# Eight sample rows as the third instead of the second tile in the last stage of a decoder layer

## What is computed

```python
x = layer_norm(DN_ALPHA * x + ffn, lw['ln2_g'], lw['ln2_b'])
ple = jax.nn.sigmoid(x @ lw['w_ple_gate']) * (p.astype(x.dtype) @ lw['w_ple_proj'])
x = x + rms_norm(ple, lw['ple_norm_g'])
```

## Time and profile before

| | us |
|---|---|
| median of 3 runs | 970.74 (970.61 to 971.94) |
| profiled execution: time | 969.24 |
| profiled execution: span | 967.4 |
| TensorE busy in the span | 928.9 |
| VectorE busy | 427.4 |
| ScalarE busy | 246.9 |
| last stage, from the first turn to the end of the span | 893.2 to 967.4 |

### The profile page before, as it was taken

One profiled execution on the slowest core, in us unless ns is written; L12 is line 12 of the kernel. 1 busy time (PEld: TensorE's weight loads), 2 busy tenths in 40 slices (PEclk: granted clock), 3 DMA queues, 4 the chain that ended last, 5 costly groups with the idle time before them and its releaser, 6 DMA issues.

```text
span 967.4 us, 13929 instructions
## 1 busy us (share of the span) xinstructions
PE 928.9 (96%) x5256; PEld 553.3 (57%) x5256; DVE 427.4 (44%) x981; ACT 246.9 (26%) x531; POOL 96.8 (10%) x146
## 2 busy tenths in 40 slices
PE   8999999999999999999999999989999999897997
PEld 6777777777777766655678645443333333233344
DVE  0311467867634238687631243682111211013784
ACT  1122221132145015665730000131111111011335
POOL 0111211211211100000000000001221111110000
PEclk9999999999999999999999999999999999899999
DMA  9876888998797711011114892348999999999501
GB/s 374 340 250 230 283 310 308 327 335 291 274 350 256 277 44 47 28 39 42 66 32 171 348 422 103 136 176 325 421 422 422 423 423 426 421 418 363 220 24 65
DMA packets 65418, 247.38 MB, mean 256 GB/s; under 512 B 11302, under 2 KB 12207, under 8 KB 56359
## 3 DMA queue, kind: packets, MB, share of 16 engines
q1 hardware_dynamic: 46742, 191.29, 50.8%
q0 software_dynamic: 13216, 35.28, 10.0%
q10 hardware_dynamic: 5392, 19.93, 5.4%
HBM read 240.85 MB, written 18.05 MB: 268 GB/s over the span
## 4 chain that ended last, share of the span: by engine, by line
PE 76%; DMA 13%; DVE 6%; ACT 2%; issue 1%; SPq 1%; DVEq 0%; ACTq 0%; POOLq 0%
PE ps L902 20%; DMA arena<-in_wexp 10%; PE ps L1371 8%; PE ps L1291 6%; PE ps L1393 4%; PE ps L1220 4%; PE ps L990 3%; PE ps L961 3%; PE ps L1075 3%; PE ps L893 3%; PE ps L1496 3%; PE ps L1099 2%; PE ps L1039 2%; PE ps L1056 1%; PE ps L965 1%; PE ps L1505 1%
## 5 line engine op out<-in xcount | busy, mean ns | idle before, releaser
L902 PE MATMUL ps<-arena 128*128 128x260 f32 x928 | 214.3, 386 | 2.2 <-DMA arena<-in_xT 1.7
L902 PEld LDWEIGHTS ps<-arena 128*128 128x128 f32 x928 | 172.7, 190 | 37.2 <-issue 8.8
L1371 PE MATMUL ps<-arena 128*64 128x512 f32 x576 | 129.2, 601 | 9.7 <-DMA arena<-in_wexp 8.1
L1371 PEld LDWEIGHTS ps<-arena 128*64 128x64 f32 x576 | 42.1, 138 | 84.3 <-issue 81.8
L1869 DVE SCALAR_TENSOR_TENSOR arena<-arena,vec 128x512 f32<-128x512 f32 x120 | 81.7, 745 | 0.0
L2550 POOL DMA_DIRECT2D arena<-in_kv x96 | 51.7, 539 | 264.9 <-issue 258.8
L1393 PE MATMUL ps<-arena 128*64 128x512 f32 x288 | 65.8, 598 | 4.1 <-DMA arena<-in_wexp 4.1
L2376 DVE TENSOR_TENSOR arena<-ps,arena 128x256 f32<-128x256 f32 x18 | 7.6, 425 | 127.3 <-ACT arena L1727 127.3
L1291 PE MATMUL ps<-arena 128*128 128x512 f32 x128 | 58.4, 601 | 0.0
L1220 PE MATMUL ps<-arena 128*128 128x260 f32 x224 | 49.3, 382 | 0.0
L1220 PEld LDWEIGHTS ps<-arena 128*128 128x128 f32 x224 | 42.6, 190 | 6.5
(11 more groups left out here) (356 smaller groups left out, 1146.2 us busy)
## 6 DMA issues: line engine op xcount, KB each, us to landing
arena<-in_wexp SPq DMA_DIRECT2D x26, 2048.0 KB, 26.3
arena<-in_kv SPq DMA_DIRECT2D x160, 272.0 KB, 9.4
arena<-in_wexp SPq DMA_DIRECT2D x36, 1024.0 KB, 27.3
arena<-in_kv POOLq DMA_DIRECT2D x96, 272.0 KB, 7.4
arena<-in_w ACTq DMA_DIRECT2D x35, 512.0 KB, 7.4
arena<-in_wexp SPq DMA_DIRECT2D x16, 512.0 KB, 10.8
arena<-in_wo SPq DMA_DIRECT2D x8, 512.0 KB, 3.8
arena<-in_w_out SPq DMA_DIRECT2D x4, 1024.0 KB
```

The lines of the kernel that those rows point to most:

```text
L902: y = mm(ps[:, b + h, 0:TH], w[:, k], xT[:, k, h * TH:(h + 1) * TH], start=(k == 0), stop=(k == KD - 1))
L1371: y = mm(ps[64 * x:64 * x + 64, 2, :], xgT[:, k, 64 * x:64 * x + 64], wx[slot][:, x, k * 512:(k + 1) * 512], start=(k == 0), stop=(k == KD ...
```

## The change

The order becomes `ORDER2 = [0, 1, 4, 2, 3]`: place 1 is the full tile 1, place 2 the sample rows. On TensorE the first tile's last chunk is followed by the full product of place 1, with the next turn before its chunk 6; `narrow` is done for place 2, with `turn_x2(3)` straight behind it; and `narrow_sum` goes before chunk 4 of place 3, into banks 0 and 1 where it was 2 and 3. On VectorE the copy to `nparts` moves from before `last(0)` to behind `gated(1)`. ScalarE's and SyncE's code is the same; what they handle follows `ORDER2`, the loads too.

```diff
-ORDER2 = [0, 4, 1, 2, 3]
+ORDER2 = [0, 1, 4, 2, 3]
...
-                if u >= 2 and u != 3:
+                if u >= 3:
+
                     pe.wait_ge(s_hg, u - 1)
-                if u == 1:
-                    narrow(6, lambda k: fbT[:, 1, k, 0:32], lambda k: plg[k]).then_inc(s_np, 1)
-                    turn_x2(2)
+                if u == 2:
+                    narrow(6, lambda k: fbT[:, 0, k, 0:32], lambda k: plg[k]).then_inc(s_np, 1)
+                    turn_x2(3)
                 elif u < TILES - 1:
...
-                        if k == KD // 2 and u == 2:
+                        if k == KD // 2 and u == 3:
                             pe.wait_ge(s_npc, 1)
-                            narrow_sum(2, nparts, 1).then_inc(s_h, 1)
-                        if k == KD - 2 and u >= 2:
+                            narrow_sum(0, nparts, 1).then_inc(s_h, 1)
+                        if k == KD - 2 and u > 0:
                             turn_x2(u + 1)
-                        if k == 0 and u == 3:
-                            pe.wait_ge(s_hg, 2)
...
             gated(0)
-            dve.wait_ge(s_np, 1)
-            v.tensor_copy(nparts, ps[:, 6:8, :].rearrange("p h n -> p (h n)")).then_inc(s_npc, 1)
             last(0)
             front(3)
             gated(1)
+            dve.wait_ge(s_np, 1)
+            v.tensor_copy(nparts, ps[:, 6:8, :].rearrange("p h n -> p (h n)")).then_inc(s_npc, 1)
             last(1)
```

## The result

The changed kernel takes 982.14 us (median of 4 runs, 981.14 to 982.44), the kernel before 970.67 us in the runs beside it. The ratio is 1.0127, with a 95% interval from 1.0114 to 1.0141: it is slower by 12.3 us (11.1 to 13.7). Executions of one kernel spread by some us, and their mean granted clock with them: of 31 executions of the kernel before on one chip, those with a mean clock of 0.992 took 967.63 to 969.43 us, those with 0.987 took 971.95 to 973.61 us. The forecast was 978.6 with 974.5 to 981.0. The direction was right; the time lies outside the range, and the loss is half as large again as the 7.9 us forecast.

The account below looks back on a forecast made before the run. TensorE, busy 96% of the span, was taken as the bound, so only its waits count: 2.9 + 4.4 + 1.2 - 1.8 = 6.7 (6.8 by path), plus 1.1 clock, +7.9 us; forecast 978.6, range 974.5 to 981.0.

Parts of the forecast that it names:

- The removed breaks: At the third tile, TensorE's old waits of 0.64 and 1.17 us go, a gain of 1.8 us.
- The second front waits for a full tile: VectorE's `front(1)` starts at 902.9 instead of 899.94 behind big loads; TensorE waits 2.9 us before the second tile's turn.
- The fourth front hangs on the third turn: `squares(0)` queues behind `turned(2)`, delaying `front(3)`: TensorE waits 4.4 us before the fourth tile's turn, 1.2 behind it.
- What is late next: At the last turn `front(4)` has a reserve of 1.3 us: no wait, and the moved copy costs nothing.
- The clock: TensorE's granted clock likely falls at the second new break: +1.1 us, between 0 and 1.6; 0 for the first.
- Rival (b): The clock falls fully at both new breaks: +10.0 us, 980.7; chance 0.17.
- (a): The second tile's big load pair lands early, near 900: +5.0, or +3.9 without the clock, 974.6 to 975.7; chance 0.13.
- (c): The fourth front is not held up, as ScalarE reaches `squares(0)` before `turned(2)`: +3.0 us, 973.7; chance 0.03.
- (d): The change does nothing, its waits only changing place and summing to zero: 970.7; chance 0.02.

Follow-up runs that it names:

- cut_loads: Changed kernel, with the second tile's two result loads bringing a quarter of each row (2 x 128 KB for 2 x 512 KB): 977.92 us, 9.1 above before.
- before_big_first: Kernel before, with the third tile's results (2 x 512 KB) loaded ahead of the sample rows' (2 x 32 KB): 973.97 us, ratio 1.0042.
- changed_again: The changed kernel timed and traced once more without any edit: 982.44 us, ratio 1.0141 to the kernel before.
- squares_first: Changed kernel, with `squares(0)` put before `turned(2)` on ScalarE: 973.89 us, ratio 1.0044 to the kernel before.
- fill_both: Changed kernel, with small matmuls on constants filling TensorE's breaks at the second and fourth tiles' turns: 976.59 us, 7.0 us above before.
- half_second: Changed kernel with the first break filled and only 4 small matmuls (1.9 us) before the fourth tile's turn: 979.52 us, ratio 1.0105 to before.

## Why the prediction was wrong

**The removed breaks** (1.8 us): right. The second tile's copies are covered, and no wait stands between 912.16 and 937.43 but the one forecast.

**The second front waits for a full tile** (+2.9 us): right in mechanism, 3.59 measured. `cut_loads` shows it by the size of the loads and `before_big_first`, in the times, by their order. That the start came so near (903.66 for 902.9) is in part luck. SyncE issued the loads at 897.19, 2.1 us later than in the earlier trace rows, because TensorE's last product ahead of the stage was 2.1 us later; and the later big load landed 6.0 us after issue instead of 6.9. In `changed_again` they were issued at 893.77, and the front started 8.3 us behind that, at 902.08: an issue 3.4 us earlier brought a start only 1.6 us earlier.

For the same pair the fit of the Trainium skill (DMA: Bandwidth & Descriptors, section "Anatomy of one DMA — SWDGE (gpsimd) path": 2.0 us and the bytes at 436 GB/s) gives, as an estimate, 4.4 us. The trace doesn't agree: the pair landed at 903.6, some 6.4 us after the first of its two issues.

**The fourth front hangs on the third turn** (4.4 us, plus 1.2 behind it): right, 4.23 and 1.18, with `squares(0)` just behind the sample tile's copies as forecast, and shown by `squares_first`.

**What is late next**: right. No wait came at the last turn, and the tail is unchanged (13.97 us for the last 48 records, as in the earlier trace rows).

**The clock** (+1.1 us): this is the step that failed. It put 1.1 us for the second break, "between 0 and 1.6", and 0 for the first. Measured were 2.7 and 1.7 us in the changed kernel's trace, 4.4 in all, and the difference between the changed kernel and `fill_both` in the times is 5.3 us. Of the 4.0 us by which the trace (11.9 us) lies above the forecast (7.9), 3.3 are this term, the waits are 0.4 and the stage's later start 0.3. The term was mis-sized in three ways. The first break was held safe because one of 3.2 us had passed; it fell. The bound of 1.6 us came from one place, where the clock had already been low for over 3 us of waiting when the matmuls came back. The 32 records at that place took 8.69 us in the trace before, but 9.43 in the changed kernel's and 10.05 in that of `changed_again`, where 7.09 is usual: 1.6, 2.3 and 3.0 us for one and the same break. And for the second break I took off a part "over waiting", since the two falls in the trace before had come some 2 us behind the last matmul. Here the fall came only at 938.2, 5.0 us behind it and inside the turn, so that just 1.18 us of waiting lay under the low clock, which then held for 5 us of dense matmuls. Rival (b), with falls at both breaks, had this right in kind with chance 0.17, and priced at 10.0 us it too was 2 us short, since it used the same bound.

**Rivals (a), (c), (d)** fell: the pair did not land near 900, the fourth front was held up, and nothing covered the waits.

Two slips in the working change nothing: the last tile's matmuls started at 947.30 before, not 947.4, which makes the sum of the path 6.9 us; and rival (c), at 973.7, is counted as no change, though 3.0 us more is outside the 1.9 us that the prediction itself allows for that.

## What to carry to other kernels

When tiles of different size change places on a saturated engine, follow every hand-written order through: here a step of another engine (`squares(0)`) stood behind a copy whose trigger the change moved 11 us later (914.73 to 926.04), and swapping two lines was worth 8 us. Price a new break on TensorE not by its length alone: add what the clock costs behind it, from several places of the trace, and let the range reach to the largest of them for each break. Put the tile with little data first in the load queue if TensorE waits for the next front.

## What was unexpected in the hardware

- The granted clock's low stretch in the changed kernel's trace lasted from 910.9 to about 914.3 behind the first break, but from about 938.2 to 945.0 behind the second, 5 us of it under dense matmuls. Sixteen records of the same kind took 7.13, 8.68, 8.80, 9.60 and 9.67 us in the traces here.
- A break of 2.30 us, a turn and 1.17 us more made the clock fall (`half_second`), and one of 3.2 us with matmuls on both sides did not the earlier trace rows. The break before 875 passed at 2.20 us in the kernel before and brought a fall at 2.00 us in the changed one.
- Small matmuls on constants held the clock at 1.00 and gave back 4 to 5 us, without making any wait longer.
